# The expert_v stage of a float32 block kernel: two chunks of a round multiplied as seven block products instead of eight

## What is computed

```python
u = expert_u[idx]
act = jax.nn.gelu(jnp.einsum('td,thkd->thk', xc, u).astype(jnp.float32), approximate=False)
w = (g * act).astype(h.dtype)
return jnp.einsum('thk,thkd->td', w, expert_v[idx])
```

## Time and profile before

| | |
|---|---|
| median of 3 runs | 1720.45 us (1718.86 to 1721.94) |
| the profiled execution | 1720.27 us, its span 1718.4 us |
| PE busy | 1685.3 us, 98% of the span |
| DVE, ACT, POOL busy | 961.0, 902.1 and 1023.5 us |
| granted TensorE clock, mean | 0.997 of full speed |
| HBM read | 285.01 MB |

### The profile page before, as it was taken

How to read it: one execution, slowest core, us unless ns; L and a number is a source line. 1 busy time by engine, 2 the same in 40 slices (tenths; PEclk the granted TensorE clock), 3 DMA queues, 4 the chain that set the end, 5 groups by cost and what they waited for, 6 DMA issues and landing times.

```text
span 1718.4 us, 29498 instructions
## 1 busy us (share of the span) xinstructions
PE 1685.3 (98%) x9320; PEld 1432.7 (83%) x9320; DVE 961.0 (56%) x2062; ACT 902.1 (52%) x1638; POOL 1023.5 (60%) x549
## 2 busy tenths in 40 slices
...
GB/s 225 177 97 133 203 158 183 183 187 183 166 160 155 157 157 193 191 192 193 195 193 190 224 138 158 74 50 165 187 191 188 179 179 140 85 179 195 186 193 123
DMA packets 83073, 288.18 MB, mean 168 GB/s; under 512 B 9264, under 2 KB 9264, under 8 KB 82480
## 3 DMA queue, kind: packets, MB, share of 16 engines
...
q10 hardware_dynamic: 432, 1.05, 0.2%
...
HBM read 285.01 MB, written 2.10 MB: 167 GB/s over the span
## 4 chain that ended last, share of the span: by engine, by line
PE 87%; DVE 4%; ACT 3%; POOL 2%; issue 2%; DMA 1%; DVEq 0%; ACTq 0%; POOLq 0%; SPq 0%
PE acc L652 13%; PE col L955 13%; PE acc L653 13%; PE acc L654 13%; PE col L1249 7%; PE col L957 7%; PE col L1253 4%; POOL w_lo L2022 2%; PE col L689 1%; PE col L690 1%; PE col L691 1%; PE mb L969 1%; PE acc L1168 1%; PE mb L970 1%; ACT w_hi L1465 1%
## 5 line engine op out<-in xcount | busy, mean ns | idle before, releaser
L2022 POOL TENSOR_TENSOR w_lo<-w_raw,w_hi 128x1024 fp32r<-128x1024 f32 (+1 forms) x403 | 952.9, 2380 | 296.7 <-ACT w_hi L1465 274.4
L1465 ACT ACTIVATE w_hi<-w_raw 128x1024 fp32r<-128x1024 f32 (+1 forms) x539 | 565.5, 1052 | 292.1 <-PE acc L654 233.0
L955 PE MATMUL col<-hT,w_hi 128*128 128x512 f32 x1024 | 365.2, 401 | 0.0
L957 PE MATMUL col<-hT,w_lo 128*128 128x256 f32 x1024 | 287.0, 280 | 0.0
L955 PEld LDWEIGHTS col<-hT,w_hi 128*128 128x128 f32 x1024 | 192.4, 188 | 45.7
L652 PE MATMUL acc<-w_hi,W_hi 128*128 128x512 f32 x512 | 199.4, 389 | 0.4 <-ACT W_hi L1686 0.2
L653 PE MATMUL acc<-w_lo,W_hi 128*128 128x512 f32 x512 | 199.2, 389 | 0.0
L654 PE MATMUL acc<-w_hi,W_lo 128*128 128x512 f32 x512 | 199.2, 389 | 0.0
L957 PEld LDWEIGHTS col<-hT,w_lo 128*128 128x128 f32 x1024 | 193.5, 189 | 0.0
L2064 POOL TENSOR_SCALAR_AFFINE_SELECT WST<-WST 128x512 f32<-128x512 f32 x1 | 1.1, 1116 | 319.4 <-DMA WST<-in_gmlp_w 319.4
L2747 DVE TENSOR_TENSOR w_lo<-w_raw,w_hi 128x1024 fp32r<-128x1024 f32 x128 | 156.2, 1221 | 1.3 <-ACT w_hi L1465 1.3
...
## 6 DMA issues: line engine op xcount, KB each, us to landing
w_raw<-in_expert_u SPq DMA_DIRECT2D x128, 512.0 KB, 3.3
w_raw<-in_expert_v SPq DMA_DIRECT2D x128, 512.0 KB, 4.3
w_raw<-in_w_mlp SPq DMA_DIRECT2D x128, 512.0 KB, 3.3
w_raw<-in_w_in SPq DMA_DIRECT2D x24, 512.0 KB, 3.9
w_raw<-in_w_qkv_o SPq DMA_DIRECT2D x24, 512.0 KB, 4.0
w_raw<-in_w_query SPq DMA_DIRECT2D x16, 512.0 KB, 3.3
w_raw<-in_w_gate SPq DMA_DIRECT2D x16, 512.0 KB, 3.4
w_raw<-in_w_qkv_e SPq DMA_DIRECT2D x12, 512.0 KB, 3.8
```

The costliest lines, as they stand in the source:

```text
L955: mm(both, wh[:, k, :], hT[:, :, k, :], start=k == 0, stop=k == KD - 1, skip_group_check=True)
L957: m = mm(both[:, 0, :], wl[:, k, :], hT_hi[:, k, :], start=False, stop=k == KD - 1, skip_group_check=True)
L1465: f(w_hi[:, s, 0:w], w_raw[:, s, 0:w], ACT.Copy).then_inc(sem(f"hi{s}"), 1)
L2022: g.tensor_tensor(w_lo[:, s, 0:w], w_raw[:, s, 0:w], w_hi[:, s, 0:w].bitcast(F32), ALU.subtract).then_inc(sem(f"lo{s}"), 1)
```

## The change

In rounds 6 to 30 of the expert_v stage (`PAIRED` to `UNPAIRED - 1`, 25 rounds) chunks 0 and 1 of the round are multiplied together. The two chunks and the two token halves form a product of 2 x 2 blocks by 2 x 2 blocks, and Strassen's method in Winograd's form makes it of seven block products instead of eight. Four of the seven have sums of blocks as operands: `VS` (sums of the stationary blocks, 128 x 128 each) and `VT` (sums of the moving ones, 128 x 512 each). The seven products accumulate in seven banks: `acc[0..2]`, `col[0..1]`, `mb[0..1]`. Chunks 2 and 3 of each round stay as they were. Rounds 0 to 5 and 31 are unchanged.

- POOL makes the sums from `w_raw` and `act_e` (`sums`), in round r those for pair r+1, then waits for `S_lo` of that pair, and then makes `w_lo` of chunk 3 of round r, which was DVE's.
- ACT makes the hi parts (`VS_hi`, `VT_hi`), DVE the lo parts, both only after PE has finished the pair before (`paired`), since there is one buffer of each. Of chunk 0 of a pair only the first half is split.
- SP's loads of round i (from round 7 on) wait for the sums that read the slots of round i-1; the reloads at the end wait for the last pair.
- DVE combines the banks after the last pair (`pair_sums`), beside round 31.

New in SP's stream:

```diff
+                    looped = PAIRED + 1 if j == V0 else LOOPS[j]
+                    with sp.Fori(0, looped) as i:
                         for q in range(4):
                             name, kind, b = PLAN[j + q][:3]
 
                             n = i * (PLAN[j + 4 + q][2] - b) + b
                             src = ins[name][n] if kind == "col" else ins[name][bass.ds(n * P, P), :]
                             load(j + q, src, i)
+                    for i in range(looped, LOOPS[j]):
+                        sp.wait_ge(sem("t_sum"), 3 * (i - PAIRED))
+                        for q in range(4):
+                            load(j + 4 * i + q)
```

PE:

```diff
+            def v_pair(r, first=False, last=False):
+
+                s0, s1 = V0 % RING, (V0 + 1) % RING
+                a, b = slice(0, 512), slice(512, 1024)
+
+                def product(o, hi, lo, b_hi, b_lo, begin=False, end=False):
+                    mm(o[:, :], hi, b_hi, start=begin, stop=False)
+                    mm(o[:, :], hi, b_lo, start=False, stop=False)
+                    return mm(o[:, :], lo, b_hi, start=False, stop=end)
+
+                if first:
+                    pe.wait_ge(sem("u_sum"), NKEYS)
+                    pe.wait_ge(sem("gated"), STEPS)
+                    pe.wait_ge(sem("gate_kept"), STEPS)
+                pe.wait_ge(sem("W_hi"), r * 4 + 2)
+                pe.wait_ge(sem("W_lo"), r * 4 + 2)
+                chunk_in(V0, r)
+                product(col[0], W_hi[:, 0, 0:P], W_lo[:, 0, 0:P], w_hi[:, s0, a], w_lo[:, s0, a],
+                        first, last).then_inc(sem(f"used{s0}"), 1)
+                chunk_in(V0 + 1, r)
+                product(acc[0], W_hi[:, 1, 0:P], W_lo[:, 1, 0:P], w_hi[:, s1, a], w_lo[:, s1, a])
+                pe.wait_ge(sem("S_hi"), r - (PAIRED - 1))
+                pe.wait_ge(sem("S_lo"), r - (PAIRED - 1))
+                product(acc[1], VS_hi[:, 3, :], VS_lo[:, 3, :], w_hi[:, s1, b],
+                        w_lo[:, s1, b]).then_inc(sem(f"used{s1}"), 1)
+                for i, (o, n, t) in enumerate(((col[1], 1, 1), (mb[1], 0, 0), (mb[0], 2, 2))):
+                    if i % 2 == 0:
+                        pe.wait_ge(sem("T_hi"), r * 2 - (2 * PAIRED - 1 - i // 2))
+                        pe.wait_ge(sem("T_lo"), r * 2 - (2 * PAIRED - 1 - i // 2))
+                    product(o, VS_hi[:, n, :], VS_lo[:, n, :], VT_hi[:, t, :], VT_lo[:, t, :],
+                            first, last)
+                product(acc[2], W_hi[:, 1, P:2 * P], W_lo[:, 1, P:2 * P], VT_hi[:, 3, :],
+                        VT_lo[:, 3, :]).then_inc(sem("paired"), 1)
+
...
+            v_pair(PAIRED, first=True)
+            v_round(PAIRED, chunks=(2, 3))
+            with pe.Fori(PAIRED + 1, UNPAIRED - 1) as r:
+                v_pair(r)
+                v_round(r, chunks=(2, 3))
+            v_pair(UNPAIRED - 1, last=True)
+            v_round(UNPAIRED - 1, chunks=(2, 3))
+            v_round(UNPAIRED, last=True)
```

ACT:

```diff
+            def next_pair(r, first=False):
+
+                j, s = V0 + 4, V0 % RING
+                act.wait_ge(sem(f"raw{s}"), upto(f"raw{s}", (j // RING + 1 + r) * 16))
+                used(act, j - RING, r)
+                f(w_hi[:, s, 0:512], w_raw[:, s, 0:512], ACT.Copy).then_inc(sem(f"hi{s}"), 1)
+                split(j + 1, r)
+                if first:
+                    used(act, V0 + 1, r)
+                    act.wait_ge(sem("W_lo"), SUMS_OVER)
+                else:
+                    act.wait_ge(sem("paired"), r - (PAIRED - 1))
+                f(W_hi[:, 0:2, :], act_e[:, bass.ds(r * 4 + 4, 2), :], ACT.Copy).then_inc(
+                    sem("W_hi"), 2)
+                act.wait_ge(sem("s_sum"), r * 3 - 3 * (PAIRED - 2))
+                f(VS_hi[:, :, :], VS[:, :, :], ACT.Copy).then_inc(sem("S_hi"), 1)
+                for i in range(2):
+                    act.wait_ge(sem("t_sum"), r * 3 - (3 * PAIRED - 4 - 2 * i))
+                    f(VT_hi[:, 2 * i:2 * i + 2, :], VT[:, 2 * i:2 * i + 2, :], ACT.Copy).then_inc(
+                        sem("T_hi"), 1)
+
+            def paired_round(r, first=False):
+
+                split(V0 + AHEAD, r)
+                gated_hi(r, 2)
+                gated_hi(r, 3)
+                next_pair(r, first)
+                split(V0 + 6, r)
...
+            paired_round(PAIRED - 1, first=True)
+            with act.Fori(PAIRED, UNPAIRED - 1) as r:
+                paired_round(r)
+            act.wait_ge(sem("paired"), PAIRS_V)
+            v_round(UNPAIRED - 1)
+            v_round(UNPAIRED, count=2)
```

POOL:

```diff
+            def sums(r, first=False):
+
+                c = r * 4 + 4
+                a = [act_e[:, c, :].rearrange("p (a s) -> p a s", a=2),
+                     act_e[:, bass.ds(c, 2), P:2 * P], act_e[:, c, 0:P], act_e[:, c + 1, 0:P]]
+                g.tensor_tensor(VS[:, 0:2, :], a[0], a[1], ALU.subtract).then_inc(sem("s_sum"), 1)
+
+                s0, s1 = V0 % RING, (V0 + 1) % RING
+                for q, s in enumerate((s0, s1)):
+                    pool.wait_ge(sem(f"raw{s}"),
+                                 upto(f"raw{s}", ((V0 + 4 + q) // RING + 1 + r) * 16))
+                if not first:
+                    pool.wait_ge(sem("T_lo"), r * 2 - 2 * (PAIRED - 1))
+                done = r * 3 - 3 * (PAIRED - 1)
+                halves = w_raw[:, :, :].rearrange("p r (n c) -> p (r n) c", n=2)
+                b11, b22 = 2 * s0, 2 * s1 + 1
+                g.tensor_tensor(VT[:, 0:2, :], halves[:, b22:b11 + 1:b11 - b22, :],
+                                halves[:, b11 + 1, :].unsqueeze(1).to_broadcast([P, 2, 512]),
+                                ALU.add).then_inc(sem("t_sum"), 1)
+                pool.wait_ge(sem("t_sum"), done + 1)
+                pool.wait_ge(sem("s_sum"), done + 1)
+                g.tensor_tensor(VT[:, 2, :], VT[:, 1, :], halves[:, b22, :], ALU.add).then_inc(
+                    sem("t_sum"), 1)
+                g.tensor_tensor(VS[:, 2, :], VS[:, 1, :], a[2], ALU.subtract).then_inc(
+                    sem("s_sum"), 1)
+                pool.wait_ge(sem("t_sum"), done + 2)
+                pool.wait_ge(sem("s_sum"), done + 2)
+                g.tensor_tensor(VT[:, 3, :], VT[:, 2, :], halves[:, b22 - 1, :], ALU.add).then_inc(
+                    sem("t_sum"), 1)
+                g.tensor_tensor(VS[:, 3, :], VS[:, 2, :], a[3], ALU.add).then_inc(sem("s_sum"), 1)
+
+            def paired_round(r, first=False):
+
+                sums(r, first)
+                pool.wait_ge(sem("S_lo"), r - (PAIRED - 2))
+                rest(V0 + AHEAD, r)
...
+                    pool.wait_ge(sem("W_lo"), SUMS_OVER)
+                    paired_round(PAIRED - 1, first=True)
+                    with pool.Fori(PAIRED, UNPAIRED - 1) as r:
+                        paired_round(r)
+                    gmlp_weights()
```

DVE:

```diff
+            def paired_round(r):
+
+                gated_lo(r * 4 + 2, 2)
+                gated_lo(r * 4 + 3, 3)
+                j, s = V0 + 4, V0 % RING
+                dve.wait_ge(sem(f"hi{s}"), upto(f"hi{s}", j // RING + 1 + r))
+                used(dve, j - RING, r)
+                v.tensor_tensor(w_lo[:, s, 0:512], w_raw[:, s, 0:512], w_hi[:, s, 0:512].bitcast(F32),
+                                ALU.subtract).then_inc(sem(f"lo{s}"), 1)
+                weight_lo(j + 1, r)
+                dve.wait_ge(sem("W_hi"), r * 4 + 6)
+                v.tensor_tensor(W_lo[:, 0:2, :], act_e[:, bass.ds(r * 4 + 4, 2), :],
+                                W_hi[:, 0:2, :].bitcast(F32), ALU.subtract).then_inc(sem("W_lo"), 2)
+                dve.wait_ge(sem("S_hi"), r - (PAIRED - 2))
+                v.tensor_tensor(VS_lo[:, :, :], VS[:, :, :], VS_hi[:, :, :].bitcast(F32),
+                                ALU.subtract).then_inc(sem("S_lo"), 1)
+                for i in range(2):
+                    dve.wait_ge(sem("T_hi"), r * 2 - (2 * PAIRED - 3 - i))
+                    n = slice(2 * i, 2 * i + 2)
+                    v.tensor_tensor(VT_lo[:, n, :], VT[:, n, :], VT_hi[:, n, :].bitcast(F32),
+                                    ALU.subtract).then_inc(sem("T_lo"), 1)
+                weight_lo(V0 + 6, r)
...
+            def pair_sums():
+
+                dve.wait_ge(sem("paired"), PAIRS_V)
+                dve.wait_ge(sem("x_back"), 16)
+
+                def add(src, t, n, sign):
+                    c = slice(n * 512, (n + 1) * 512)
+                    then(v.scalar_tensor_tensor(out=XB[:, t, c], in0=src[:, :], scalar=sign / GATE,
+                                                in1=XB[:, t, c], op0=ALU.mult, op1=ALU.add))
+
+                then(v.tensor_copy(VE[:, :], col[0][:, :]))
+                add(col[0], 0, 0, 1.0)
+                then(v.tensor_tensor(VE[:, :], mb[0][:, :], VE[:, :], ALU.add))
+                add(VE, 0, 1, -1.0)
+                add(col[1], 0, 1, 1.0)
+                add(col[1], 1, 1, 1.0)
+                then(v.tensor_tensor(VE[:, :], mb[1][:, :], VE[:, :], ALU.add))
+                add(VE, 1, 0, 1.0)
```

(11 more changed lines are left out.)

23 lines of the change are left out of this document (14 added, 9 removed).

## The result

The changed kernel takes **1918.41 us** (median, 1914.7 to 1923.46), the kernel before 1719.97 beside it: ratio 1.1156, 95% interval 1.1142 to 1.1169, slower by 198 us. Forecast were 1881 with a range of 1825 to 1930: the sign and the mechanism came as written, the size was 37 us short.

A forecast was written before the change was run, and what follows sets the result against it. PE bounds the kernel before; the change makes a loop through POOL and the load queue bound it. 24 periods of 17.3 us after 708.8, plus 28.4, end the stage 161 us later: 1881 us, range 1825 to 1930.

The forecast's parts named there:

- The loop: In paired rounds, POOL's w_lo of chunk 3, three loads, sums, S_hi, S_lo and w_lo again set a 17.3 us period.
- R(5): End of POOL's w_lo of chunk 3 in round 5, the first late one, forecast at 708.8 us.
- Load leg: From POOL's w_lo end: 0.23 us to the load's issue, then 6.6 for three 512 KB loads to land, plus handover.
- Sums: POOL's sums for the next pair, after the loads: one over 1024, two over 512, two over 128, 5.92 us.
- The rest of the loop: After the sums: S_hi on ACT 0.60 us, S_lo on DVE 0.69, w_lo on POOL 2.40, with handovers of 0.14 each.
- The final sums on DVE lie beside round 31 and cost nothing: At the stage's end, nine DVE operations, 6.3 us, were to hide beside 10.9 us of PE work.
- R(29): End of POOL's w_lo of chunk 3 in round 29, forecast 24 periods of 17.3 us after 708.8.
- ACT and DVE get about 2 us more work per round each: In paired rounds, both engines, half idle before, were to hide about 2 us more work each.
- PE's stand: PE was to idle some 7 us before chunk 3 in each period, its clock probably sinking each time.
- PE cold in all of the loop: Rival: PE's clock stays at half through the paired rounds, period 18.9 us, time 1920; chance 0.10.
- The chain over S_lo alone: Rival: loads not late, only pair's end, S_hi, S_lo, w_lo set the period, 12.3 us, time about 1759; chance 0.08.
- Hidden: Rival: all added work is hidden, saved matmuls bring 17.0 us, the transition costs 2, time 1705; chance 0.05.

The follow-up runs named there:

- experiments 1: The changed kernel with POOL's wait for S_lo moved behind its w_lo of chunk 3: 1884.42 us.
- experiment 2: The changed kernel with the loads of the next pair's chunks 0 and 1 put ahead of the load of chunk 3: 1844.61 us.
- experiment 8: The kernel before plus 60 unneeded POOL operations with two SBUF operands over 1024 elements in the expert_v stage: 1744.74 us.
- Kernels 6: The changed kernel with sums and all w_lo on DVE, none on POOL, and 13 pairs, in every second round: 1715.84 us.
- 10: The changed kernel with sums on DVE, 12 pairs in every second round, final sums in two pieces, XB reloaded ahead of round 29's weights: 1714.45 us.
- 12: The changed kernel with sums on DVE, 16 pairs, final sums in two pieces, XB reloaded in four pieces behind weight loads: 1709.31 us.
- experiment 3: The changed kernel with the next pair's loads ahead of chunk 3's and POOL's wait for S_lo behind its w_lo: 1833.90 us.

## Why the prediction was right, and where its size was off

- *The loop.* POOL's w_lo, load queue, three loads, sums, S_hi, S_lo, w_lo: right in every link, in the chain above, and by experiments 1 and 2, which take two links out and get 1.3 and 2.8 us a round back. R(5) was 711.7 for 708.8.
- *Load leg.* Issue, three loads and a handover were priced at 0.23 + 6.6 + 0.14 = 6.97; from 912.00 to 918.48 it is 6.48. The Trainium skill, "DMA: Bandwidth & Descriptors", section "Anatomy of one DMA — SWDGE (gpsimd) path", has a rule that makes three loads 5.6 us, an estimate, as in the forecast; it is given for loads issued by GpSimd, and these are SP's. From 912.07 to 918.33 they took 6.26, so the rule came out 0.7 too short here.
- *Sums: the term that was mis-sized.* 5.92 + 0.28 = 6.20 priced, 7.53 measured (918.48 to 926.01). The operations over 1024 and 512 took 2.41 and 1.34 as priced, but the second over 512 took 1.56 and the two over 128 0.65 and 1.43, for 0.46. The rows that priced them came from stretches without such a neighbour (from 300 to 640 us DVE's costliest operations beside POOL read PSUM); here DVE made W_lo and w_lo beside them at two to five times their length, and the engines held each other up. In experiment 2, where DVE stood at that moment, the same operations took 1.28 and 0.46; experiment 8 shows the taking of turns by itself. That the range held it is in part luck: the sums ran 1.33 us over, more than the tenth for slower POOL operations in its upper end (0.83), and the room came from that end's 7.6 for the loads, which took 6.26.
- *The rest of the loop.* S_hi, S_lo, w_lo with handovers 4.11 priced, 3.89 measured. Sum for this turn 17.9 for 17.3; the mean over 24 is 18.16, other turns being longer in the same terms. 24 x 0.88 = 21 of the 37 us.
- *"The final sums on DVE lie beside round 31 and cost nothing"*: wrong, by 6.8 us. PE ends the stage at about 1177.2; the residual starts at 1184.01, right behind PE before. The sums could begin only at 1174.08: DVE's queue stood 5.58 us for a W_hi of ACT's, and ACT for the first chunk of the next stage, whose load was queued behind the reloads. Kernels 6, 10 and 12 show that this tail is there with fewer pairs and can be taken away.
- *The balance.* The span is 197.7 us longer, forecast was 161. R(5) gives 2.9 of the 36.7 between them, the loop 20.6 (24 x 18.16 for 24 x 17.3), PE's work behind R(29) 1.3 (29.7 for 28.4), the residual 6.8: 31.6. Between the residual and the first load of w_out_e (1260.0, before 1061.1) another 6.1 are lost; the 8 us at 0.50 would be 4 of them by the halved clock, an estimate, and the rest was not traced; 1.2 come back later. That the late residual brought this clock on was not tried by itself.
- *"ACT and DVE get about 2 us more work per round each, that alone is hidden"*: true here only because the loop was longer, and the T sums' lo parts, priced within 3.6 us of S_hi, came at R + 2.7 (914.75), still ahead of PE's use. Of a 10.2 us round DVE's part, with POOL's turns in between, is too much: at a period of 14.72 DVE and POOL are busy for 0.89 and 0.83 of the time (experiment 3).
- *PE's stand.* Some 7 us were forecast before each chunk 3, 5.5 measured on average: the first nine to twelve matmuls behind each gap come 0.43 us apart, not 0.23, and PE's busy part of the longer period grows by some 2 us.
- *Rivals.* PE cold in all of the loop did not come: the clock falls to 0.50 in every gap, which the Trainium skill, "TensorE: Matmul & The Clock Gate", section "HAM oscillation — how this bites in real kernels", has too, but is back at 1.00 6 us behind R in the loop, where PE has slack until the next. The chain over S_lo alone (12.3) falls in the changed kernel itself, where POOL's first sum waits for the load in each of 17 turns (83.3 us); and with the loads out of the way the period is still 15.32 (experiment 2). Hidden: never near.
- *Where the gain of 17 us went.* It was there on PE (75 matmuls fewer), and could not be had on POOL in any order that was tried. On DVE, whose operations are half as long, 16 of 25 pairs fit, and pay 10.9.
